# Two projections of a decoder layer interleaved at the start, and the gate broadcast put behind the last projection

## The reference, cut to what matters

```
mod = silu(c) @ w_ada + b_ada;  shift, scale, gate = split(mod, 3)
h   = rms_norm(x, norm_w) * (1 + scale) + shift
u_a, v_a, z_a, q_b, k_b, v_b, z_b = split(h @ w_in, 7)      # each 512 wide
a_out = u_a * (tril(w_s) @ rms_norm(v_a) + b_s) * silu(z_a)  # chunks of 128 positions
q, k  = rope(rms_norm(q_b)), rope(rms_norm(k_b))
b_out = rms_norm(diff_attention(q, k, v_b)) * (1 - lambda_init) * silu(z_b)
x     = x + gate * (concat(a_out, b_out) @ w_out)
```

## Time and profile before

| | |
|---|---|
| median of 3 runs | 656.74 us (656.07 to 656.80) |
| the profiled execution | 657.29 us |
| its span on the slowest core | 656.2 us |
| spans of the 8 cores | 647.9 to 656.2 us |
| PE busy | 516.3 us (79%) |
| DVE busy | 380.0 us (58%) |
| ACT busy | 331.6 us (51%) |
| POOL busy | 33.9 us (5%) |

### The profile page before, as it was taken

The page is one execution under the profiler, slowest core; times in us unless marked ns, Lnnn a source line. Parts: engine busy times, 40 slices in busy tenths (PEclk is TensorE's granted clock), DMA queues, the critical chain, the costliest instruction groups (busy, mean ns, idle before and its releaser), DMA issues.

```text
span 656.2 us, 8577 instructions; the slowest of 8 cores (647.9 to 656.2 us)
## 1 busy us (share of the span) xinstructions
PE 516.3 (79%) x2688; PEld 210.4 (32%) x2688; DVE 380.0 (58%) x662; ACT 331.6 (51%) x452; POOL 33.9 (5%) x54
## 2 busy tenths in 40 slices
PE   0011669999999999989878888788888898979980
PEld 0000224444434334444323333233322233334430
DVE  2238484567288786448825556655555556665445
ACT  1231625653377677412267777777766677710000
POOL 2000000000000000000000001100000000100000
PEclk9999979999999999989979999999988899989995
DMA  8999920337220403210080000000000000035667
GB/s 217 304 307 252 267 37 12 54 96 161 39 26 1 65 0 46 52 33 1 0 129 1 0 1 1 2 0 1 1 0 1 1 1 1 1 129 177 204 220 233
DMA packets 21677, 50.52 MB, mean 77 GB/s; under 512 B 1424, under 2 KB 8848, under 8 KB 21632
## 3 DMA queue, kind: packets, MB, share of 16 engines
q1 hardware_dynamic: 12656, 39.22, 19.1%
q0 software_dynamic: 8976, 10.75, 11.4%
HBM read 51.34 MB, written 8.39 MB: 91 GB/s over the span
## 4 chain that ended last, share of the span: by engine, by line
PE 49%; DMA 16%; DVE 15%; ACT 10%; issue 9%; DVEq 1%; SPq 0%; ACTq 0%; POOLq 0%
PE psum L659 16%; PE psum L618 8%; ACT sb_regA L893 7%; DMA sb_qT<-w_adaT 6%; PE psum L905 6%; PE psum L908 5%; PE psum L870 4%; DVE sb_regD L563 4%; DMA sb_regC<-w_in 3%; PE psum L979 3%; DMA out<-sb_regD 3%; DMA sb_regD<-x 3%; PE psum L877 2%; PE psum L711 2%; DVE sb_regB L918 2%
## 5 line engine op out<-in xcount | busy, mean ns | idle before, releaser
L893 ACT ACTIVATE sb_regA<-psum,sb_small 128x1024 bf16<-128x1024 f32 x144 | 158.1, 1110 | 44.4 <-PE psum L870 22.7
L659 PE MATMUL psum<-sb_hT,sb_regC 128*128 128x512 bf16 x640 | 150.9, 387 | 23.6 <-DMA sb_regC<-w_in 18.4
L905 PE MATMUL psum<-sb_regA,sb_constb 128*128 128x512 bf16 (+1 forms) x288 | 109.0, 379 | 12.8 <-ACT sb_regA L893 11.7
L908 PE MATMUL psum<-sb_regA,sb_vB 128*128 128x512 bf16 (+1 forms) x288 | 107.3, 378 | 0.0
L659 PEld LDWEIGHTS psum<-sb_hT,sb_regC 128*128 128x128 bf16 x640 | 62.7, 99 | 95.9 <-issue 31.0
L870 PE MATMUL psum<-sb_qT,sb_kT 64*128 64x256 bf16 (+1 forms) x576 | 61.7, 273 | 25.1 <-DVE sb_regB L828 20.9
L618 PE MATMUL psum<-sb_regC,sb_hT 128*128 128x512 bf16 x256 | 56.7, 379 | 0.0
L870 PEld LDWEIGHTS psum<-sb_qT,sb_kT 64*128 64x128 bf16 x576 | 19.5, 94 | 85.8 <-issue 82.3
L413 PE MATMUL psum<-sb_vB,sb_constb 128*128 128x512 bf16 x32 | 10.8, 504 | 45.1 <-ACT sb_vB L406 45.1
L918 DVE COPY sb_regB<-psum 128x512 f32<-128x512 f32 x32 | 22.0, 687 | 41.8 <-PE psum L908 41.6
L905 PEld LDWEIGHTS psum<-sb_regA,sb_constb 128*128 128x128 bf16 x288 | 28.2, 98 | 51.0 <-issue 35.5
(11 more groups left out here) (128 smaller groups left out, 609.5 us busy)
## 6 DMA issues: line engine op xcount, KB each, us to landing
sb_regD<-x SPq DMA_DIRECT2D x16, 512.0 KB, 5.4
sb_qT<-w_adaT SPq DMA_DIRECT2D x15, 512.0 KB, 13.7
sb_regC<-w_in POOLq DMA_DIRECT2D x7, 1024.0 KB, 10.2
sb_regD<-w_adaT SPq DMA_DIRECT2D x9, 512.0 KB, 11.9
out<-sb_regD SPq DMA_DIRECT2D x8, 512.0 KB, 3.6
out<-sb_regA SPq DMA_DIRECT2D x8, 512.0 KB, 3.5
sb_szb<-xT SPq DMA_DIRECT2D x1, 2048.0 KB, 20.7
sb_kT<-xT SPq DMA_DIRECT2D x1, 2048.0 KB, 23.2
```

Of the source, the lines that this page charges most:

```text
L659: P.op("pe", lambda E, kc=kc: E.matmul(PS(bank), lhsT=wslot[ws_][:, kc, 128 * c4:128 * (c4 + 1)], rhs=hT[:, kc, cols], start=(kc == 0), st ...
L893: P.op("act", lambda E: E.activation(out=et, in_=psum[:, X:X + 2, :], func=AF.Exp, bias=negM, scale=0.125), reads=[pb[X], pb[Y], b_small], ...
L905: P.op("pe", lambda E, rhs=rhs, st=st, dview=dview: E.matmul(dview, lhsT=ones_b, rhs=rhs, start=st, stop=False, skip_group_check=True), re ...
L908: P.op("pe", lambda E, rhs=rhs, st=st, vt=vt, oview=oview: E.matmul(oview, lhsT=vt, rhs=rhs, start=st, stop=False, skip_group_check=True), ...
```

## The change

`phaseB` gives four columns to DVE and four to ACT. ZA is the second group; its first eight tiles (blocks 0 and 1) run between U's blocks 1 and 2, the other eight behind U's block 3. `phaseM` and `phaseB` of block 2 are issued behind U's block 1, those of block 3 behind ZA's block 0. VA's weights are loaded behind U's last tile. As ZA uses the `tm` buffers while `rstdx4[2]` and `rstdx4[3]` are needed, these two move to another part of `regD`. `late_setup` now comes behind U and ZA. `gate_broadcast` moves from between ZA and ZB to behind the last group.

```diff
-    rstdx4 = [uz_f[:, 0:512], regD[:, 2048:2560], regD[:, 2560:3072], regD[:, 3072:3584]]
+    rstdx4 = [uz_f[:, 0:512], regD[:, 2048:2560], regD[:, 0:512], regD[:, 512:1024]]
...
-    b_rstdx4 = [buf("rstdx4_0"), b_st[1], b_tm[0], b_tm[1]]
+    b_rstdx4 = [[buf("rstdx4_0")], [b_st[1]], [b_sq[0], b_sq[1]], [b_qc[0], b_qc[1]]]
...
         for kc in range(KC):
-            if kc < 7:
+            if kc < 4:
                 P.op("dve", lambda E, kc=kc: E.tensor_scalar(
...
-    order = [G_U, G_VA, G_VB, G_Q, G_K, G_ZA, G_ZB]
+    order = [G_U, G_ZA, G_VA, G_VB, G_Q, G_K, G_ZB]
...
-        if gi + 1 < len(order) and gi >= 1:
+        if gi + 1 < len(order) and gi >= 2:
             load_w(gi + 1)
...
         elif g == G_U:
-            for tb in range(TB):
-                if tb + 1 < TB:
-                    if tb + 1 >= 2:
-                        phaseM(tb + 1, "dve")
-                    phaseB(tb + 1)
+            phaseB(1)
+            for tb in (0, 1):
                 for c4 in range(4):
-                    step(make_tile(gi, g, (c4, tb)))
+                    step(make_tile(0, G_U, (c4, tb)))
                 if tb == 0:
                     phaseA_rest(2)
                     phaseA_rest(3)
+            phaseM(2, "dve")
+            phaseB(2)
+            for tb in (0, 1):
+                for c4 in range(4):
+                    step(make_tile(1, G_ZA, (c4, tb)))
+                if tb == 0:
+                    phaseM(3, "dve")
+                    phaseB(3)
+            for tb in (2, 3):
+                for c4 in range(4):
+                    step(make_tile(0, G_U, (c4, tb)))
+            load_w(2)
+            for tb in (2, 3):
+                for c4 in range(4):
+                    step(make_tile(1, G_ZA, (c4, tb)))
             drain()
             late_setup()
+        elif g == G_ZA:
+            pass
...
-        if g == G_ZA:
-            drain()
-            gate_broadcast()
         checkpoint("g%d" % g, locals())
     drain()
+    gate_broadcast()
```

More of the change, by code:

```diff
@@ L416, in phaseA_rest @@
         P.op("act", lambda E: E.activation(out=rstdx4[tb], in_=PS(bank), func=AF.Ln, bias=epsn, scale=1.0 / D),
-             reads=[pb[bank], b_small], writes=[b_rstdx4[tb]])
+             reads=[pb[bank], b_small], writes=b_rstdx4[tb])
         P.op("act", lambda E: E.activation(out=rstdx4[tb], in_=rstdx4[tb], func=AF.Exp, scale=-0.5),
-             reads=[b_rstdx4[tb]], writes=[b_rstdx4[tb]])
+             reads=b_rstdx4[tb], writes=b_rstdx4[tb])
     def phaseA(tb):
@@ L428, in phaseM @@
                                             in1=rstdx4[tb].unsqueeze(1).broadcast_to([128, KC, 512]), op=ALU.mult),
-             reads=xs_b[s_] + [b_rstdx4[tb]], writes=xs_b[s_])
+             reads=xs_b[s_] + b_rstdx4[tb], writes=xs_b[s_])
     def phaseB(tb):
@@ L666, in s1 @@
                 P.op("act", lambda E: E.activation(out=uz[:, c4, cols], in_=PS(bank), func=AF.Copy),
-                     reads=[pb[bank]], writes=[b_uz, b_junk, b_rstdx4[0]])
+                     reads=[pb[bank]], writes=[b_uz, b_junk] + b_rstdx4[0])
             T["s1"] = s1
```

## The result

The changed kernel takes 675.37 us (median of 10 runs, 674.09 to 676.84) against 656.12 (10 runs): ratio 1.0289, 95% interval 1.0271 to 1.0307. It is 19.3 us slower.

The account below looks back on a forecast made before the run. It took a chain half TensorE, with DMA, DVE and ACT behind, as the bound. 3.6 + 9.6 - 4.1 + 9.4 = 18.5 on 657.29 gave 675.8, less 0.55 for the median: 675 us; range 664 less 1 to 682.

Parts of the forecast that it names:

- Part 1: U and ZA interleaved, phaseB split at 4: the old hole shrinks, a longer one appears; 3.6 us slower.
- PE's hole: In ZA, PE waits 7.8 us for a Silu behind block 3's ACT columns, as phaseM(3) starts late, at 99.6.
- the small one: In ZA, the old 5.2 us hole is left as a 0.9 us PE wait for a bank.
- ACT's column: ACT's four phaseB columns per block, about 0.72 us each, 2.97 for four, standing behind DVE's four.
- Rival B: In U and ZA, PE has enough banks and runs without a hole: -7.6 for +3.6, 664 us; chance 0.08.
- Part 2: late_setup behind ZA: rope chain exposed before the first unfold, 7.3 us, plus 2.3 for the clock; 9.6 slower.
- Part 3: K meets ZB directly: 4.1 us gained; a clock drop from PE's wait at chunk 1, 0 to 2, not summed.
- Part 4: Gate broadcast between ZB's last chunk and attention: second exponential 9.4 us later, bounds 8.6 to 9.9.
- The second sum in the prediction, 678: Two newly exposed table switches, Silu before phaseM(3) and Exp behind the gate, cost 2.8 us more by the page.
- Rival C: Waiting instructions on ACT or DVE don't hold those behind; rope and gate hide, 645 us; chance 0.04.
- rival D: Small waits in ZA (0.9) and chunk 1 (2.9) drop the clock, attention starts slower: 4 to 6 more, 680; chance 0.07.
- Rival E: Whole change does nothing: holes trade one for one, rope and gate stay covered, 657 us; chance 0.02.

Follow-up runs that it names:

- run 3: Changed kernel with phaseM(3) issued right behind phaseB(2), ahead of ZA's products on DVE, phaseB(3) left in place: 669.43 us, ratio 1.0171 to the kernel before.
- run 4: Changed kernel with phaseM(3) ahead of ZA's products and phaseB(3) behind ZA's block 1: 665.62 us, ratio 1.0117 to the kernel before.
- run 5: Changed kernel with phaseB split again at seven columns for DVE and one for ACT: 670.81 us, ratio 1.0264 to the kernel before.
- run 2: Changed kernel with rope's DVE work behind the first tile of U's block 2, its sines before ZA's block 2: 663.91 us, ratio 1.0102 to the kernel before.
- run 6: Kernel before with only the gate broadcast moved behind ZB: 658.02 us, ratio 1.0071 to the kernel before.
- run 1: Changed kernel with the gate broadcast moved from behind ZB into VB's tiles 11 to 15: 662.54 us, ratio 1.0076 to the kernel before.
- run 7: Kernel before with only the gate broadcast moved into VB's tiles 11 to 15: 650.99 us, ratio 0.9948 to the kernel before.
- run 10: Changed kernel with gate in VB, rope under U, phaseM(3) and phaseB(3) moved, plus five of 16 gmlp chunks in VB: 659.10 us, ratio 1.0015 to before.
- run 9: Changed kernel with gate in VB and rope under U's block 2, phaseM(3) and phaseB(3) left as changed: 658.36 us, ratio 1.0007 to before.

## Why the prediction was right

**Part 1,** 3.6 expected, 3.4 measured (U and ZA 71.5 forecast from U's first matmul, 72.0 measured; the forecast started from one core's 40.3 for the old U, where the mean is 41.0). The chain went as told: M3 behind the third product (99.6 forecast, 100.6 on this core's clock if its later start is taken off), PE's hole 7.8 forecast, 8.1 measured, 0.9 forecast for the small one, 1.4 measured on this core and none to 1.4 on the others. Behind the hole the 136 matmuls took 31.28, 1.8 more than 136 x 0.216 + 0.16, where 2.3 stood for the clock. The term that was short is ACT's column: 0.82 with 0.09 between them, 3.55 for four where I had 2.97. Runs 3 and 4 show that both links, DVE's order and ACT's, make the hole; run 5 that the even split lengthens it. Rival B is out: three banks did not carry PE over.

**Part 2,** 7.3 + 2.3 expected, 6.0 + 2.8 measured. The first was too large by a table load: I carried 1.28 us over from U, where Ln and Exp stood ahead of the Sine. Behind ZA's Silus the Sine has no ACT_TABLE_LOAD ahead of it in the trace. The Trainium skill, ScalarE: Activation LUTs, Table sets: the hidden batching unit, says that tables come as named sets of several functions; that these two share one is what the missing row shows. What the clock took after the rope's wait is 2.0 by run 2.

**Part 3,** -4.1 expected, -2.6 measured: the wait of 3.0 at chunk 1 did drop the clock (0.72 in the window), which stood in the text as 0 to 2 and outside the sum. On the two cores whose rows are shown it is -3.2 (69.6 and 38.8), and there chunks 1 and 2 take 5.6 us (306.98 to 312.56) where two at 2.43 are 4.9, so the clock is most of what is missing. The means are closer together, as two cores of before take 68.3 for this stage. What the one number -4.1 did not tell apart, run 6 does: the gain is all the gate's, and K meeting ZB directly costs about 4 us.

**Part 4,** 9.4 expected, 9.4 measured, and 10.0 by the fifth exponential (it starts at 360.35, 15.9 us behind the last chunk, and at 338.51, 5.8 behind it, before), since the products of the first exponential are behind as well. Runs 1, 6 and 7 show it by itself. The window of 345 to 351 has the clock at 0.50, the slower pace that I took. The second sum in the prediction, 678, had a drain at each of the two newly exposed table loads; from the start of the load to the first ACTIVATE it is 1.30 us in both places (97.31 to 98.61, 351.63 to 352.93), so neither shows one.

**The rest.** The terms of the traces make 3.4 + 6.0 + 2.8 - 2.6 + 9.4 = 19.0 for 18.5 forecast. That the median came out at 675.4 for 675 is closer than the terms are: the one too large (table load) and those too small (the clock at chunk 1, ACT's columns) cancel, which is luck. Rival C can't hold after runs 1 to 4: in each, moving an instruction in a queue, and nothing else, gave the time back. Of rival D's two clock losses the one at chunk 1 was there and is part of the 2.6; the one behind the small wait in ZA was not (1.00 in the window from 97.5). Rival E's cover was not there: PE had nothing to do under the rope, nor attention under the gate.

## What to carry to other kernels

Work put in to fill a hole brings its evacuations with it, and these stand in the same in-order queues as the prologue that made the hole: look at what each engine has queued ahead of the next link, not at how busy it is. Small serial pieces (a broadcast, a table of angles) are free only where another engine has work over them; when a stage moves, ask for each such piece what lay over it, and place it in a stage where both of its engines have slack. And where two engines hand small pieces to each other, interleave no second chain of the same two between them (run 10). Last, measure a new order against the old one with the same repairs: run 9 looks level with the kernel before, and is 3.9 us slower than that kernel with its gate in VB (run 7).

## What was not expected of the hardware

The same short pause does not always cost the clock. At K's start PE waits in three pieces, 0.88 + 0.49 + 0.31 us, on core 7 of the changed kernel (tile at 257.02), and at the same place as long on core 1 (tile at 259.19). Windows of core 7, then core 1: over the pause, and behind it.
```profile
253.00:257.00 4.00, 2.32 (x10) 0.73 (x9) 3.00 (x8) 2.12 (x4) 0.28 (x1) 1.00 0.80 113
257.00:261.00 4.00, 4.00 (x19) 1.68 (x18) 3.08 (x5) 2.92 (x5) 0.00 (x0) 1.00 0.95 151
```
```profile
256.00:259.20 3.20, 1.52 (x7) 0.37 (x6) 2.70 (x5) 1.92 (x3) 0.00 (x0) 1.00 0.52 72
259.20:262.20 3.00, 3.00 (x10) 1.17 (x9) 1.64 (x3) 1.80 (x3) 0.00 (x0) 0.60 1.07 98
```
One stays at 1.00, the other runs at about half behind the pause. The same three waits stand at K's start in all runs, so the profiled cores can be counted. Where they add up to 1.4 us (0.61 + 0.49 + 0.31; nine kernels, the one before among them) the clock is at 1.00 behind them on all 72 cores. Where they add up to 1.65 to 1.69 it is down on 1 of 8 cores in the changed kernel, on 2, 2 and 1 in runs 2, 3 and 4, and on 7 of 8 in run 7. There the tile behind the pause takes 3.18 us on core 1 for 1.89 on core 2, and the seven cores take 151.5 to 151.7 from the first unfold to K's end, the eighth 150.0: so it costs 1.5 us. In a sum such a pause is a chance and not a term, and these runs don't say what sets the chance.

The hole of the rope has a chance of this kind as well. Of the changed kernel's cores four take 149.6 to 150.0 us from the first unfold to K's end and four 151.0 to 151.2 (in the kernel before all eight take 147.7 to 147.8). On one of the four slow ones, core 1, the clock fell at K's start; on the other three it stayed down longer behind the rope's wait. Windows of the changed kernel's core 0, then core 2:
```profile
157.00:159.00 2.00, 2.00 (x9) 0.91 (x8) 0.72 (x2) 1.33 (x4) 0.00 (x0) 1.00 0.00 0
```
```profile
157.00:159.00 2.00, 2.00 (x6) 0.98 (x4) 0.78 (x2) 1.32 (x3) 0.00 (x0) 0.50 0.00 0
```
Their unfolds start within 0.3 us of each other (153.01, 153.29). What stays open is the last column, which differs by up to 3.6 us between versions (315.6 to 319.2) though nothing in it was changed.
